# Hybrid window-attention and retention layer: stacked retention queries, x split before its norm, GroupNorm affine on ScalarE

## What is computed

```python
h = rms_norm(x, norm_gain)
proj = jnp.einsum('bsd,de->bse', h, w_in)
aq, ak, av, ag, rq, rk, rv, rg = jnp.split(proj, SPLIT_POINTS, axis=-1)
attn = window_attention(...)      # 16 heads of 64, 4 kv heads, window of 2 chunks of 64, QK norm, ALiBi, sinks
ret = retention(...)              # 8 heads, q/k 64 wide, v 128 wide
mixed = jnp.concatenate([attn * jax.nn.silu(ag), ret * jax.nn.silu(rg)], axis=-1)
x = x + jnp.einsum('bse,ed->bsd', mixed, w_out).astype(x.dtype)

# retention, per chunk: decayed intra-chunk part, and the state r carried across chunks
intra = jnp.einsum('bnhij,bnjhe->bnihe', a, vc)
cross = jnp.einsum('bnihd,ih,nbhde->bnihe', qc, wq, r_prev)
o = (intra + cross).reshape(b, s, RET_HEADS, RET_V_DIM)
mu = jnp.mean(o, axis=-1, keepdims=True)
var = jnp.mean(jnp.square(o - mu), axis=-1, keepdims=True)
o = (o - mu) * lax.rsqrt(var + EPS)
```

## Time and profile before

| | |
|---|---|
| median of 3 runs | 1611.86 us (1611.46 to 1613.65) |
| the profiled execution, its own time | 1613.94 us |
| its span on the core | 1612.1 us, 24573 instructions |
| TensorE matmuls, busy | 1571.5 us (97%), 8208 instructions |
| TensorE weight loads | 1370.7 us (85%) |
| VectorE | 1139.9 us (71%), 3040 instructions |
| ScalarE | 654.8 us (41%), 1892 instructions |
| GpSimd | 482.8 us (30%), 477 instructions |
| mean granted TensorE clock | 0.995 |
| DMA | 324.67 MB, 201 GB/s over the span |
| chain that ended last | TensorE 78%, VectorE 16%, issue 3% |

### The profile page before, as it was taken

How to read it: one execution, slowest core, us unless ns; L and a number is a source line. 1 busy time by engine, 2 the same in 40 slices (tenths; PEclk the granted TensorE clock), 3 DMA queues, 4 the chain that set the end, 5 groups by cost and what they waited for, 6 DMA issues and landing times.

```text
span 1612.1 us, 24573 instructions
## 1 busy us (share of the span) xinstructions
PE 1571.5 (97%) x8208; PEld 1370.7 (85%) x8208; DVE 1139.9 (71%) x3040; ACT 654.8 (41%) x1892; POOL 482.8 (30%) x477
## 2 busy tenths in 40 slices
PE   4999999999899999999999999999999999999998
PEld 4897888988789889898888988889898898988887
DVE  6798686796965757568694775857788575675864
ACT  4655455454433434333443342433343343333430
POOL 4564675655512022120421202122140211202210
PEclk9999999999999999999999999999999999999999
DMA  8776766774855536445357444546356554353451
GB/s 287 263 274 239 273 251 245 261 258 152 302 213 200 195 118 245 159 158 219 126 227 264 176 175 166 187 162 234 133 195 217 188 219 176 121 214 120 182 209 53
DMA packets 123020, 324.67 MB, mean 201 GB/s; under 512 B 16784, under 2 KB 57872, under 8 KB 122896
## 3 DMA queue, kind: packets, MB, share of 16 engines
q1 hardware_dynamic: 122896, 323.10, 55.0%
HBM read 251.75 MB, written 71.30 MB: 200 GB/s over the span
## 4 chain that ended last, share of the span: by engine, by line
PE 78%; DVE 16%; issue 3%; ACT 1%; DMA 1%; POOL 0%; SPq 0%; DVEq 0%; ACTq 0%; POOLq 0%
PE jb L1327 22%; PE jb L1328 22%; PE jb L1329 22%; PE ob L1387 2%; PE ptb L1373 2%; PE s L1364 2%; DVE xt L1042 1%; DVE oraw L1003 1%; PE ob L1346 1%; DVE rawqn L858 1%; DVE qS L867 1%; DVE mixr L931 1%; PE s L1421 1%; DVE rawqn L855 1%; PE s L1422 1%
## 5 line engine op out<-in xcount | busy, mean ns | idle before, releaser
L1327 PE MATMUL jb<-wH,hTH 128*128 128x512 f32 (+1 forms) x1024 | 377.5, 369 | 12.6 <-DVE hTL L804 12.6
L1328 PE MATMUL jb<-wL,hTH 128*128 128x512 f32 (+1 forms) x1024 | 374.2, 365 | 0.0
L1329 PE MATMUL jb<-wH,hTL 128*128 128x512 f32 (+1 forms) x1024 | 373.9, 365 | 0.0
L1327 PEld LDWEIGHTS jb<-wH,hTH 128*128 128x128 f32 x1024 | 194.4, 190 | 32.0 <-DVE hTL L804 12.0
L1329 PEld LDWEIGHTS jb<-wH,hTL 128*128 128x128 f32 x1024 | 194.2, 190 | 20.5
L1328 PEld LDWEIGHTS jb<-wL,hTH 128*128 128x128 f32 x1024 | 194.4, 190 | 18.1
L1327 PE MATMUL jb<-wH,mxH 128*128 128x512 f32 x512 | 208.8, 408 | 0.0
L1327 PE MATMUL jb<-hTH,wH 128*128 128x512 f32 x512 | 201.4, 393 | 0.7 <-POOL wL L360 0.7
L1329 PE MATMUL jb<-wH,mxL 128*128 128x512 f32 x512 | 201.2, 393 | 0.0
L1328 PE MATMUL jb<-wL,mxH 128*128 128x512 f32 x512 | 201.2, 393 | 0.0
L1328 PE MATMUL jb<-hTL,wH 128*128 128x512 f32 x512 | 199.7, 390 | 0.0
(11 more groups left out here) (146 smaller groups left out, 2904.3 us busy)
## 6 DMA issues: line engine op xcount, KB each, us to landing
wH<-scrH SPq DMA_DIRECT2D x144, 512.0 KB, 7.0
wL<-scrL SPq DMA_DIRECT2D x144, 512.0 KB, 7.9
stage<-wp_dram SPq DMA_DIRECT2D x48, 512.0 KB, 6.2
scrH<-wH SPq DMA_DIRECT2D x48, 512.0 KB, 6.1
scrL<-wL SPq DMA_DIRECT2D x48, 512.0 KB, 6.8
wH<-scrH SPq DMA_DIRECT2D x48, 384.0 KB, 5.3
wL<-scrL SPq DMA_DIRECT2D x48, 384.0 KB, 6.6
xt<-xT_dram SPq DMA_DIRECT2D x16, 512.0 KB, 5.9
```

The costliest lines, as they stand in the source:

```text
L1327: pe.matmul(o, lh, rh_, start=i == 0, stop=False)
L1328: pe.matmul(o, lh, rl_, start=False, stop=False)
L1329: m = pe.matmul(o, ll, rh_, start=False, stop=i == last)
```

## The change

In the numbering of the code, "from unit 6 on" is n >= 5 (`STACKED`).

- **Stacked queries.** A new tile `zst` holds, for head a, the high queries on that head's 64 rows and the low queries on the other 64 (`rqh` and `rqz`, two more ScalarE copies each). `rst2` holds the state's high part on all 128 rows and its low part on the head's own 64 rows, zeros on the others (`rh`: 4 ScalarE copies in place of 1; `rl`: 2 subtractions in place of 1). `I` then has one state matmul for a head (256 columns) where it had two (256 and 128 columns). Both tiles lie where `stage` was, which is no longer used by then. `rst` is updated in place; `rcur` and its copy in `carry_in` go.
- **x split raw.** `xh` rounds x times gain straight from the loaded x, for two of the 8 slices at a time, and `xl` subtracts on VectorE in all blocks (line 1153); `h`, `xl_first` and GpSimd's `xl` go. 1/rms is applied later: as the scale of ScalarE's copies of q, k, v, of the retention value and gate, in `kw_am`, in GroupNorm's epsilon and last product, and to the attention gate by a new VectorE product `agz`, with the factor transposed by `XB` and copied by `xrb_copy`. TensorE waits for one slice at a time, and only in the first unit of a block.
- **GroupNorm affine.** `gnb`'s two subtract-and-multiply instructions go to ScalarE (`gnx`, scale and bias), with the bias from a small VectorE product `gnm`.
- **The shifted values.** The two copies of `v_parts` to `veven` and `vcar` go to ScalarE (`v_shift`).
- **Start.** SyncE loads the gain first, then x-transposed and weights in four alternating pieces (a fourth place for weights lies in `sx`); the rows of x, the identity, the saves and the constants come later.
- **Order.** All five tables are new.

```diff
+STACKED = NU + 1
...
-        stage = sb("stage", [P, STAGES, 2, 512])
+        with nc.sbuf_tensor("stage", [P, STAGES, 2, 512], F32) as stage:
+            pass
+        zst, rst2 = sb("zst", [P, 2, BLK], F32R), sb("rst2", [P, 2, 2, RV], F32R)
+        sb("behind", [P, STAGES * 1024 - 1536])
...
+        def stage_of(q, w):
+            return sx[:, 0:2 * w].rearrange("p (s w) -> p s w", s=2) if q == 3 else stage[:, q % STAGES, :, 0:w]
...
+            sp.dma_start(ngain[:, :], norm_gain.rearrange("(k p) -> p k", p=P), allow_slow_non_contiguous=True
+                         ).then_inc(S["s_gains"], 16)
+            for c in range(4):
+                sp.dma_start(xt[:, 0, 2 * c:2 * c + 2], xT[0, 0, :, 2 * c:2 * c + 2]).then_inc(s_xp[c], 16)
+                load(c)
...
-                act.activation(raw[:, t % 2], bank_of(n, J_QKV + t)[:, 0:384], ACT.Copy).then_inc(S["s_raw"], 1)
+                    act.wait_ge(S["s_vol"], nth(n, 4, t - 2))
+                if n % NU == 0:
+                    act.wait_ge(S["s_xr"], nth(n // NU, 4, t))
+                act.activation(raw[:, t % 2], bank_of(n, J_QKV + t)[:, 0:384], ACT.Copy,
+                               scale=xr[:, n // NU % 2, t, 0:1]).then_inc(S["s_raw"], 1)
                 act.wait_ge(S["s_raw"], nth(n, 4, t))
...
+            def v_shift(n, t):
+                act.wait_ge(S["s_vol"], nth(n, 4, t))
+                act.activation(veven[64:128, t], vodd[0:64, t].bitcast(F32), ACT.Copy)
+                after = veven[0:64, t + 1] if t < NT - 1 else vcar[0:64, n % NU]
+                act.activation(after, vodd[64:128, t].bitcast(F32), ACT.Copy).then_inc(S["s_vev"], 1)
+
+            def gnx(n, t):
+                act.wait_ge(S["s_nb"], nth(n, 4, t))
+                for h in range(2):
+                    i = act.activation(oraw[:, t % 2, h], oraw[:, t % 2, h], ACT.Identity, bias=gnf[:, t % 2, 2 + h:3 + h],
+                                       scale=gnf[:, t % 2, h:h + 1])
+                i.then_inc(S["s_gn"], 1)
 
...
+                if n >= STACKED:
+                    act.wait_ge(S["s_i"], 4 * n)
+                    for a in range(2):
+                        rows = slice(a * 64, a * 64 + 64)
+                        i = act.activation(zst[rows, a], th[rows, :], ACT.Copy)
...
+            def rqz(n):
+                if n < STACKED:
+                    return
+                act.wait_ge(S["s_rql"], nth(n, 2, 1))
+                for a in range(2):
+                    rows, other = slice(a * 64, a * 64 + 64), slice(64 - a * 64, 128 - a * 64)
+                    i = act.activation(zst[other, a], rqL[rows, a].bitcast(F32), ACT.Copy)
+                i.then_inc(S["s_rqz"], 1)
...
             def rh(n, t):
...
+                if n < STACKED:
+                    act.activation(rHL[:, 0], rst[:, n % NU], ACT.Copy).then_inc(S["s_rh"], 1)
+                    return
...
+                for a in range(2):
+                    for half in range(2):
+                        i = act.activation(rst2[half * 64:half * 64 + 64, a, 0], rst[a * 64:a * 64 + 64, n % NU], ACT.Copy)
+                i.then_inc(S["s_rh"], 1)
...
             def xrb_copy(b):
 
-                act.wait_ge(S["s_xb"], nth(b, 4, 3))
-                act.wait_ge(S["s_qn"], nth(b * NU - 1, 4, 3))
-                act.activation(xrb, ab[:, :], ACT.Copy).then_inc(S["s_xrb"], 1)
...
+                act.wait_ge(S["s_xb"], b + 1)
+                if b:
+                    act.wait_ge(S["s_agz"], 2 * NU * b)
+                act.activation(xrb[:, :], ab[:, :], ACT.Copy).then_inc(S["s_xrb"], 1)
...
+            def xh(b, t, c):
...
+                for k in (2 * c, 2 * c + 1):
+                    act.activation(hTH[:, k, t * P:(t + 1) * P], xt[:, t % 2, k], ACT.Copy, scale=ngain[:, k:k + 1]
+                                   ).then_inc(S["s_xH"], 1)
...
+            def agz(n, i):
+                v.wait_ge(S["s_job"], JOB_DONE[n, J_AG + i])
+                if n % NU == 0 and i == 0:
+                    v.wait_ge(S["s_xrb"], n // NU + 1)
+                if n:
+                    v.wait_ge(S["s_mixr"], 4 * n)
+                v.tensor_tensor(gate[:, i * 512:(i + 1) * 512], bank_of(n, J_AG + i)[:, :], xrb[:, :], ALU.mult
+                                ).then_inc(S["s_agz"], 1)
...
             def rl(n, t):
...
+                for a in range(2):
+                    rows, other = slice(a * 64, a * 64 + 64), slice(64 - a * 64, 128 - a * 64)
+                    if n == STACKED and t == 0:
+                        v.memset(rst2[other, a, 1].bitcast(F32), 0.0)
+                    i = sub(rst2[rows, a, 1], rst[rows, n % NU], rst2[rows, a, 0])
+                i.then_inc(S["s_rl"], 1)
...
+            def gnm(n, t):
+                v.wait_ge(S["s_grs"], nth(n, 4, t))
+                v.scalar_tensor_tensor(out=gnf[:, t % 2, 2:4], in0=mv[:, :, 0], scalar=-1.0, in1=gnf[:, t % 2, 0:2],
+                                       op0=ALU.mult, op1=ALU.mult).then_inc(S["s_nb"], 1)
 
             def gnb(n, t):
 
-                v.wait_ge(S["s_grs"], nth(n, 4, t))
+                v.wait_ge(S["s_gn"], nth(n, 4, t))
                 v.wait_ge(S["s_ggm"], nth(n, 4, t))
-                for h in range(2):
-                    i = v.tensor_scalar(oraw[:, t % 2, h], oraw[:, t % 2, h], mv[:, h, 0:1], grs[:, h:h + 1], ALU.subtract, ALU.mult)
-                link(i)
-                v.tensor_tensor(oraw[:, t % 2], oraw[:, t % 2], gg[:, t % 3].rearrange("p (h e) -> p h e", h=2), ALU.mult
-                                ).then_inc(S["s_mr"], 1)
+                v.scalar_tensor_tensor(out=oraw[:, t % 2], in0=oraw[:, t % 2], scalar=xr[:, n // NU % 2, t, 0:1],
+                                       in1=gg[:, t % 3].rearrange("p (h e) -> p h e", h=2), op0=ALU.mult, op1=ALU.mult
+                                       ).then_inc(S["s_mr"], 1)
...
-                for k in range(KT):
-                    i = v.scalar_tensor_tensor(out=xt[:, t % 2, k], in0=xt[:, t % 2, k], scalar=ngain[:, k:k + 1],
-                                               in1=factor, op0=ALU.mult, op1=ALU.mult)
...
+            def xl(b, t, c):
+                for k in (2 * c, 2 * c + 1):
+                    v.wait_ge(S["s_xH"], 32 * b + 8 * t + k + 1)
+                    cols = slice(t * P, (t + 1) * P)
+                    v.scalar_tensor_tensor(out=hTL[:, k, cols], in0=xt[:, t % 2, k], scalar=ngain[:, k:k + 1],
+                                           in1=hTH[:, k, cols].bitcast(F32), op0=ALU.mult, op1=ALU.subtract
+                                           ).then_inc(S["s_xL"], 1)
...
-                    if j < J_AG and i == KT // 2:
-                        pe.wait_ge(S["s_xL"], nth(n // NU, 8, 2 * j + 1))
+                    if j < J_AG and n % NU == 0:
+                        pe.wait_ge(S["s_xL"], 8 * NT * (n // NU) + 8 * j + i + 1)
...
+                if n >= STACKED:
+                    pe.wait_ge(S["s_rqz"], n - STACKED + 1)
...
-                    pe.matmul(o, rqH[:, a, cols], both(rHL[:, :, :]), start=True, stop=False)
+                    if n < STACKED:
+                        pe.matmul(o, rqH[:, a, cols], both(rHL[:, :, :]), start=True, stop=False)
+                        pe.matmul(o[:, 0:P], rqL[:, a, cols], rHL[:, 0], start=False, stop=False)
+                    else:
+                        pe.matmul(o, zst[:, a, cols], both(rst2[:, a]), start=True, stop=False)
                     pe.matmul(o, aH[:, e], both(v), start=False, stop=False)
-                    pe.matmul(o[:, 0:P], rqL[:, a, cols], rHL[:, 0], start=False, stop=False)
                     pe.matmul(o[:, 0:P], aL[:, e], v[:, 0], start=False, stop=True)
...
+            def XB(b):
+
+                if b == 0:
+                    pe.wait_ge(S["s_ident"], 16)
+                ab_free()
+                ab_user[0] = ("s_xrb", b + 1)
+                for t in range(NT):
+                    pe.wait_ge(S["s_xr"], nth(b, 4, t))
+                    m = pe.transpose(ab[:, t * P:(t + 1) * P], xr[:, b % 2, t, 0:1].broadcast_to([P, P]), ident[:, :])
+                m.then_inc(S["s_xb"], 1)
```

1047 lines of the change are left out of this document (536 added, 511 removed).

## The result

The changed kernel takes 1589.4 us (median of 4 runs, 1588.5 to 1592.0), the kernel before on the same chip 1611.7 (1610.8 to 1613.7): ratio 0.986, 95% interval 0.985 to 0.988. That is 22.3 us gained where 30.7 were forecast.

A forecast was written before the change was run, and what follows sets the result against it. TensorE was taken as the bound from 440 to 1600 us, waits before that. Gains 10.2 + 11 + 3 + 6.5 = 30.7 us from 1613.94 give 1583.2, as median 1581; 8 in 10: 1566 to 1596.

The forecast's parts named there:

- Part 1: State product: one matmul for two removes 88 small matmuls at 0.116 us each, 10.2 us gained.
- So nothing on the path: State's way between successive `I`: it grows by about 1.2 us, within 2.5 us of cover, so it costs nothing.
- The cover of 2.5 us: Slack before the next `I`: the state's low part was done at 695.06, `I` began at 697.55.
- the state's way becomes the bound: Rival on `rh` and `rl` in strict queues: at 3.5 us more per tile, 44 tiles lose 1 us each, 1625; chance 0.03.
- Part 2: Kernel start up to job 8: TensorE 17 to 21 us late in place of 30.5, taken as 11 us gained.
- the 4 us for collisions: Kernel start: allowance between 17 and 21 us late, for VectorE instructions slowed beside GpSimd subtractions.
- the start is hidden: Rival at the start: weights' splitting sets the pace, collisions hold every `xl`; only 5 us gained, 1587; chance 0.13.
- Part 3: Units 1 to 3, 60 to 400 us: half of TensorE's 6.0 us idle time taken back, 3 us.
- Part 4: First block turn: VectorE is late, GpSimd loses its subtractions of x; 6.5 us of 8.7 taken back.
- the 8.7: First block turn: the us it cost more than the second in the kernel before.
- Costed at nothing: ScalarE's other new work, 7.4 us a unit, `agz` and the unchanged end: no cost expected.
- The signs: Expected in the trace: 88 fewer matmuls, eight steps of `I`, idle under 6 us from 60 to 440, block period 386.6.

The follow-up runs named there:

- e2: The kernel before, with the matmul of the low query part left out from unit 5 on (88 small matmuls, that output term missing): 1603.4 us, ratio 0.995.
- e1: The changed kernel with the state matmuls unstacked in every unit, so 88 small matmuls come back and the order stays: 1592.2 us, ratio 0.988.
- e6: The changed kernel with GpSimd's subtractions of the first unit's gate and value-gate panels cut from 512 to 64 columns: 1581.7 us, ratio 0.981.
- e8: The changed kernel with the GroupNorm's affine on VectorE again, two instructions per tile, off ScalarE: 1595.0 us, ratio 0.989.
- e7: The kernel before, with GpSimd's eight subtractions of x of the second block cut from 512 to 32 elements each: 1604.8 us, ratio 0.995.

## Why the prediction was right, and where it was not

Direction and range were right (1589.4 in 1566 to 1596), the point 8.4 us too low. Two terms failed and two came in near or above their size; that the total still lies in the range is in part luck and owes something to the turn, which gave more than was forecast while the stacking and the start gave less.

- **Part 1, the matmuls: right in its price, wrong in its cover.** 0.116 us a matmul held: `I` went from 1.28 to 1.05 us, and e2 shows it with nothing else changed. Of the two sections of the Trainium skill's TensorE: Matmul & The Clock Gate, the traces side with LDWEIGHTS (107 ns) and not with the isolated gap of Back-to-back issue gap (56 ns). "So nothing on the path" is the step that failed. The cover of 2.5 us was read between the first and second tile of the old order, and up to the state's low part alone; `aL`, for which `I` waits too, ended there at 695.60, which leaves 1.95. The new order puts one job, not two, between the third and the fourth, and there 0.2 us were left. Of 9.0 us of shorter `I`, 5.2 came back as late starts; net it is worth 2.8 (e1), under the 7 us that I had named as the sign of being wrong, and the waits of `I` after 440 us were the other sign. So the rival "the state's way becomes the bound" was there, at 0.48 us in nine units instead of 1 us in 44 tiles, and through `aL` at the end of VectorE's queue rather than through the state itself.
- **Part 2, the start: 6.5 us by the two traces (4.5 by the trace of e2), not 11.** The steps up to the gate panel were near: first matmul 8.11 for 7.1, first transposes 26.60 for 26.5, last gate slice 42.0 for 38 to 42. What failed is job 8, which ended at 72 and not at 66 to 70; TensorE was 23 us late there and 24.4 behind the next wait, and not 17 to 21. The term that was too small is the 4 us for collisions. With GpSimd's subtractions of the gate and value panels short, lateness is 16.9 and the kernel 7.7 us faster (e6), but how much of that is collisions and how much the slices' own pace isn't told apart. The size is near that of the rival "the start is hidden", but the collisions were not where it put them: seven `xl` of the first job took 1.09 us each, where the slices set the pace anyway, the 22 after them 0.34 to 0.35. Held were VectorE's small instructions, 0.95 us in place of 0.16, between 28 and 74 us.
- **Part 3, units 1 to 3:** 3.8 us for 3. By e8, 0.6 us of it is the affine's move.
- **Part 4, the first turn: 8.2 to 8.9 us for 6.5.** The direction was argued from GpSimd's queue, and e7 bears it out: cutting its subtractions of x gives 7 of the 8.7. I took 6.5 of the 8.7, since VectorE kept its own eight instructions a tile; nearly all of it came. Part of the 8.7 was the price of the lower clock behind the 3.74 us wait, which went with the wait and which I had not counted by itself.
- **"Costed at nothing"** held for ScalarE's work in the steady units, where TensorE waits for none of it. It missed the last unit: `I` of its third tile waits 1.1 us for `kwL`, a wait that is not there unstacked (e1), and behind `PV(14, 3)` 3.1 us in all were given back.
- **The signs.** Matmuls and steps of `I`: as said. Idle from 60 to 440 us 4.8, under 6. The block period was to be 386.6 us: the `I` of the third tile lies at 785.64 in unit 7 and at 1173.50 in unit 11, 387.9 apart: four late starts of about 0.5 between them, less the wait of 0.66 that the kernel before had at the second turn.

## What to carry to other kernels

When an edit makes a chain longer and also comes with a new order, read the cover of that chain in the new order, tile by tile, at the place where the least work stands between producer and user, and up to the last of the values for which the user waits (here `aL`, not the state); the removed work itself makes the consumer arrive sooner. A step that saves time on the bound engine is worth only what the next queue lets through: the same stacking was worth 2.8 us in one order and 8.0 in another. Waits at a start or a turn are best priced by shortening the suspected instruction (e6, e7), since one held engine hides behind another.
